# Eighteen down-projection units as seven block products instead of eight

## The reference

```python
# first block, per layer:
h = h + 0.5 * swiglu(rmsnorm(h, ffn1_norm), w_gate, w_up, w_down)       # D_FF = 2816
h = h + mixer(rmsnorm(h, mix_norm))
h = h + 0.5 * swiglu(rmsnorm(h, ffn2_norm), w_gate, w_up, w_down)
# second block, per layer:
mix = mixer_sublayer(x, ...)
x = layer_norm(DEEPNORM_ALPHA * x + mix, ln1_g, ln1_b)
ff = jnp.square(jax.nn.relu(x @ w_ff1)) @ w_ff2                         # D_FF_2 = 4096
x = layer_norm(DEEPNORM_ALPHA * x + ff, ln2_g, ln2_b)
```

## Time and profile before

| | |
|---|---|
| median of three runs | 2044.6 us |
| span of the profiled execution | 2042.5 us (the runs' median is 2.1 us above it) |
| PE busy | 2034.5 us, 10364 instructions |
| PE weight load busy | 1718.3 us |
| DVE busy | 1389.1 us |
| ACT busy | 1018.4 us |
| POOL busy | 92.8 us |
| granted TensorE clock | 1.000 of full speed |

### The profile page before, as it was taken

How to read it: one execution, slowest core, us unless ns; L and a number is a source line. 1 busy time by engine, 2 the same in 40 slices (tenths; PEclk the granted TensorE clock), 3 DMA queues, 4 the chain that set the end, 5 groups by cost and what they waited for, 6 DMA issues and landing times.

```text
span 2042.5 us, 25162 instructions
## 1 busy us (share of the span) xinstructions
PE 2034.5 (100%) x10364; PEld 1718.3 (84%) x10364; DVE 1389.1 (68%) x1624; ACT 1018.4 (50%) x1290; POOL 92.8 (5%) x133
## 2 busy tenths in 40 slices
PE   9999999999999999999999999999999999999998
PEld 7888888888888888888888888888888888888887
DVE  6655687775757566877675667757767677577675
ACT  6444576453445335775443365644444466445331
POOL 1001010000010001100100000000100000000000
PEclk9999999999999999999999999999999999999999
DMA  9655554465566656544656474555755656455552
GB/s 333 211 187 166 178 162 141 167 214 185 186 197 210 194 168 201 165 145 145 226 191 197 153 242 155 166 172 173 239 186 189 204 153 194 156 185 193 196 189 83
DMA packets 225569, 377.73 MB, mean 185 GB/s; under 512 B 6592, under 2 KB 113216, under 8 KB 225456
## 3 DMA queue, kind: packets, MB, share of 16 engines
q1 hardware_dynamic: 221472, 362.64, 54.1%
q0 software_dynamic: 3984, 13.49, 2.2%
HBM read 375.05 MB, written 1.05 MB: 184 GB/s over the span
## 4 chain that ended last, share of the span: by engine, by line
PE 98%; DVE 1%; ACT 0%; issue 0%; DVEq 0%; POOL 0%; ACTq 0%; POOLq 0%
PE pb L1656 63%; PE pb L1667 18%; PE pb L1670 9%; PE pb L1679 2%; PE pb L1725 1%; PE pb L1803 1%; DVE wl L2109 0%; PE pb L1802 0%; PE pb L1790 0%; PE pb L1860 0%; PE pb L1782 0%; PE pb L1645 0%; DVE lS L2292 0%; PE pb L1649 0%; PE pb L1647 0%; PE pb L1684 0%
## 5 line engine op out<-in xcount | busy, mean ns | idle before, releaser
L1891 ACT ACTIVATE wh<-raw 128x2048 fp32r<-128x2048 f32 (+2 forms) x347 | 654.2, 1886 | 626.6 <-PE pb L1656 271.3
L2109 DVE TENSOR_TENSOR wl<-raw,wh 128x2048 fp32r<-128x2048 f32 (+2 forms) x347 | 777.3, 2247 | 149.0 <-ACT wh L1891 147.8
L1656 PE MATMUL pb<-wh,x 128*128 128x512 f32 (+1 forms) x2144 | 651.3, 385 | 0.0
L1656 PEld LDWEIGHTS pb<-wh,x 128*128 128x128 f32 x2144 | 400.7, 188 | 77.9
L1656 PE MATMUL pb<-wl,x 128*128 128x512 f32 (+1 forms) x1072 | 421.1, 393 | 0.1
L1667 PE MATMUL pb<-x,wh 128*128 128x512 f32 x1568 | 397.0, 395 | 0.0
L1667 PEld LDWEIGHTS pb<-x,wh 128*128 128x128 f32 x1568 | 283.3, 189 | 51.8
L1656 PE MATMUL pb<-wl,mh 128*128 128x512 f32 (+1 forms) x740 | 255.7, 391 | 0.0
L1656 PE MATMUL pb<-wh,ml 128*128 128x512 f32 (+1 forms) x740 | 253.7, 388 | 0.0
L1656 PE MATMUL pb<-wh,mh 128*128 128x512 f32 (+1 forms) x740 | 253.5, 388 | 0.0
L1656 PEld LDWEIGHTS pb<-wl,x 128*128 128x128 f32 x1072 | 201.4, 188 | 42.2 <-issue 3.7
(11 more groups left out here) (365 smaller groups left out, 1611.8 us busy)
## 6 DMA issues: line engine op xcount, KB each, us to landing
raw<-in_w_in_dram SPq DMA_DIRECT2D x100, 1024.0 KB, 5.3
raw<-in_w_ff_dram SPq DMA_DIRECT2D x64, 1024.0 KB, 5.3
raw<-in_ffn_w_down_dram SPq DMA_DIRECT2D x44, 1024.0 KB, 4.9
raw<-in_ffn_w_up_dram SPq DMA_DIRECT2D x42, 1024.0 KB, 5.3
raw<-in_ffn_w_gate_dram SPq DMA_DIRECT2D x41, 1024.0 KB, 5.3
raw<-in_w_branch_dram SPq DMA_DIRECT2D x24, 1024.0 KB, 5.0
raw<-in_w_out_dram SPq DMA_DIRECT2D x16, 1024.0 KB, 5.0
raw<-in_w_in_dram SPq DMA_DIRECT2D x4, 832.0 KB, 4.4
```

The source lines that it names most:

```text
L1656: ins = e.matmul(pb[b][:, 0:c1 - c0], x[:, s, cols], w[:, n, c0:c1], start=(it["first"] and n == 0 and q == 0), stop=(it["stop"] and n == ...
L1891: e.activation(hi, raw, ACT.Copy).then_inc(m.high_done, 1)
L2109: e.tensor_tensor(lo, raw, hi.bitcast(F32), ALU.subtract).then_inc(m.low_done, 1)
```

## The change

`down` marks two units of each chunk (`seven_units`) as 2x2 blocks: left operand A split in token halves by K tiles, right operand B in K tiles by column halves. In place of eight block products there are seven, of sums of blocks of B (`sum`, four 128x512 pieces, made by DVE from the raw weights, split by ACT and DVE as `sumh`, `suml`) and sums and differences of blocks of A (`diff`, made by POOL from `mn`, split as `diffh`, `diffl`). Three products go straight to the main banks, four to the side banks, which both marked units of the chunk share; then `recombine` adds the side banks to `h` (one ACT copy, eight DVE instructions). The chunks are the first of the three `ffn1` calls after the opening one, and all three of both `ffn2` calls: nine chunks, 18 units.

A `diff` needs its hidden values in `mn` in the wide form. So in `ffn2`'s first chunk the second 512 columns, before in the tokens form, are now in the wide form, and the starting group has two units instead of four.

The side operands take memory that the mixer constants use, so `loads` is now called ahead of the last group of down units.

```diff
@@ advance / new helpers
         while self.nlo < self.nhi:
-            self.add("low", j=self.nlo)
+            n = self.seven.get(self.nlo)
+            if n is not None and n > 1 and n - 2 not in self.sum_free:
+                break
+            self.add("low", j=self.nlo, n=n, after=self.sum_free.get(n - 2) if n is not None else None)
             self.nlo += 1
+            self.sum_low_next()
+            if n is not None:
+                self.sum_high_due = n
...
+    def seven_products(self, j, job):
+        n, slots = self.next("seven"), job["slots"]
+        self.seven_of[j] = n
+        self.sum_high_next()
+        self.sum_low_next()
+        need = self.need("M", slots, [0, 1]) + self.need("D", [n], [0])
...
+        v = self.pe("seven", j=j, n=n, slots=slots, mains=mains, sides=self.side_uses, first=first,
+                    begin=job["seven"] == "first", end=job["end"], need=need)
...
+        if job["end"]:
+            r = self.next("recombined", 2)
+            self.add("recombine", p=v["p"], uses=self.side_uses, coef=job["coef"], n=r,
+                     need=self.h_ready[0] + self.h_ready[1])
...
@@ split_later: after a wide product
+            if slot // 2 in self.seven_units:
+                self.mn_free[q].append(self.differences(q, ("product", n + 1)))
+    def differences(self, q, need):
+        n = self.next("diff")
+        self.add("diff", q=q, n=n, need=need, after=self.sum_free.get(n - 2))
+        def high():
+            self.add("diffhigh", n=n, after=self.sum_free.get(n - 2))
+            self.later.append(low)
+        def low():
+            self.add("difflow", n=n)
+            self.ready["D", n, 0] = ("diff_low", n + 1)
+        self.later.append(lambda: self.later.append(high))
@@ ffn1
-        if loads:
-            loads()
+            self.seven_units = () if opening or n0 else (2, 3)
-            self.down(dn, l, n0, sum(chunks) // 256, sizes, 0.5, after if n0 else None)
+            self.down(dn, l, n0, sum(chunks) // 256, sizes, 0.5, after if n0 else None, loads=loads if n0 else None)
@@ ffn2
-        if loads:
-            loads()
-            first = 2 if n0 == 0 else 0
+            self.seven_units = (2, 3) if n0 == 0 else (0, 1)
+            first = 1 if n0 == 0 else 0
-                                 last=(i == 1), epi=self.relu_t(4 * c)) for c in range(2) for i in range(2)],
+                                 last=(i == 1), epi=self.relu_t(4 * c)) for c in range(first) for i in range(2)],
@@ PE
+        elif k == "seven":
...
+            pe.wait_ge(m.low_done, it["j"] + 1)
+            pe.all_ready(it["need"])
+            for x, y, k, (b, g), first, stop in (
+                    ([x[:, s0, T] for x in a], w, 0, q1, begin, it["end"]),
+                    ([x[:, s1, T] for x in a], w, 2, q2, b2, False),
+                    ([x[:, 3, :] for x in d], w, 3, q3, b3, False),
+                    ([x[:, 1, :] for x in d], v, 0, q5, begin, it["end"]),
+                    ([x[:, 0, :] for x in d], v, 1, q7, begin, it["end"]),
+                    ([x[:, 2, :] for x in d], v, 2, q6, begin, it["end"]),
+                    ([x[:, s1, U] for x in a], v, 3, q4, b4, False)):
+                if y is v:
+                    pe.wait_ge(m.sum_low, n + 1)
+                if first:
+                    pe.wait_ge(m.evac[b], g)
+                e.matmul(pb[b][:, :], x[0], y[1][:, k, :], start=first, stop=False)
+                e.matmul(pb[b][:, :], x[0], y[0][:, k, :], start=False, stop=False)
+                ins = e.matmul(pb[b][:, :], x[1], y[0][:, k, :], start=False, stop=stop)
@@ DVE
+                v.step(e.tensor_tensor(V[:, 0:2, :], B[:, 0:4:3, :], B[:, 1:2, :].broadcast_to([P, 2, 512]), ALU.add))
+                v.own_steps()
+                v.step(e.tensor_tensor(V[:, 2, :], V[:, 0, :], B[:, 3, :], ALU.add))
+                e.tensor_tensor(lo[:, 0:512], raw[:, 0:512], hi[:, 0:512].bitcast(F32), ALU.subtract)
...
+        elif k == "recombine":
...
+            v.pe(p)
+            v.all_ready(it["need"])
+            v.wait_ge(m.part_copied, n // 2 + 1)
+            e.tensor_tensor(E, Q6, W, ALU.add).then_inc(m.evac[q6[0]], 1)
+            e.scalar_tensor_tensor(h[0][0], Q1, c, h[0][0], ALU.mult, ALU.add).then_inc(m.evac[q1[0]], 1)
...
+            e.scalar_tensor_tensor(h[1][1], E, c, h[1][1], ALU.mult, ALU.add).then_inc(m.evac[q7[0]], 1)
```

More of the change, by code:

```diff
@@ L274, in sbuf @@
         self.chunk = A("chunk", o_ck, [P, P], U32)
+        o_sum, o_sumh = (o_xn, o_g[1]), (o_lane[0], o_r2)
+        self.sum = [A(f"sum{i}", o_sum[i], [P, 4, 512]) for i in range(2)]
+        self.suml = [A(f"suml{i}", o_sum[i], [P, 4, 512], F32R) for i in range(2)]
+        self.sumh = [A(f"sumh{i}", o_sumh[i], [P, 4, 512], F32R) for i in range(2)]
+        self.diff = [A(f"diff{i}", o_r2 + 8192 + 2048 * i, [P, 4, P]) for i in range(2)]
+        self.diffl = [A(f"diffl{i}", o_r2 + 8192 + 2048 * i, [P, 4, P], F32R) for i in range(2)]
+        self.diffh = [A(f"diffh{i}", o_r2 + 12288 + 2048 * i, [P, 4, P], F32R) for i in range(2)]
+        self.mix = [A(f"mix{i}", o_xn + 2048 * i, [P, 512]) for i in range(3)]
         self.lrR = A("lrR", o_dist, [P, S], F32R)
@@ L538, in group @@
             need = self.need(X, slots, [t])
-            if job["first"]:
-                for b, _, _ in job["segs"]:
+            if job.get("seven"):
+                if t == 0:
+                    self.seven_products(j, job)
+                self.tick()
+                continue
+            first = []
+            for b, _, _ in job["segs"]:
+                first.append((t, b) not in self.opened if job["first"] is None else job["first"])
+                if first[-1]:
                     self.main_use[t, b] = self.use(2 * t + b)
+                    self.opened.add((t, b))
             segs = [(self.main_use[t, b], c0, c1) for b, c0, c1 in job["segs"]]
@@ L692, in cut, with seven @@
                 after(1, 1)
+        def seven(i):
+            return ("first" if i == min(self.seven_units) else "next") if i in self.seven_units else None
         u = 0
+        self.opened = set()
         for size in sizes:
-            first, last = u == 0, u + size == n_units
+            last = u + size == n_units
+            if last and loads:
+                loads()
             if last and after:
@@ L705, in down @@
                                  slots=[2 * (u + i), 2 * (u + i) + 1], segs=[(0, 0, 512), (1, 512, 1024)],
-                                 first=first and i == 0, last=last and i == size - 1, epi=epi)
+                                 first=None, last=last and i == size - 1, epi=epi, coef=coef,
+                                 seven=seven(u + i), end=u + i == max(self.seven_units, default=None))
                             for i in range(size)])
@@ L870, in ffn2 @@
                     n_t += 1
[L871 removed]
+            self.down("w_ff2_2", l, n0, n_chunks * 2, sizes, 1.0, after if n0 == 2560 else None, n0 == 2560 and l == L - 1,
+                      loads if n0 == 2560 else None)
     def start(self):
@@ L1644, in pe_program @@
                     pe.wait_ge(m.x0_high, 1)
-                e.matmul(pb[b][:, :], xh[:, s, cols], hi[:, 0, :], start=it["first"], stop=False)
+                e.matmul(pb[b][:, :], xh[:, s, cols], hi[:, 0, :], start=it["first"][0], stop=False)
                 pe.all_ready(it["need"])
```

135 lines of the change are left out of this document (119 added, 16 removed).

## The result

The changed kernel takes 2085.8 us (median of four runs, 2084.9 to 2086.9); the kernel before, with one run more than above, takes 2044.7. That is a ratio of 1.020 (95% interval 1.019 to 1.022), 41.1 us slower. The profiled execution has a span of 2085.1, 42.6 above that of before.

The account below looks back on a forecast made before the run. PE was taken as the bound in every stage: -13.4 us of removed work, +40.6 of waits on DVE in ffn2 and +4 of clock gave +31.2 on 2044.6, so 2076 us, range 2050 to 2092.

Parts of the forecast that it names:

- B: ffn2's second chunk, first marked unit: PE waits for diffl because DVE lags behind added work; 7.5 us a layer.
- the second part of D: ffn2's third chunk: the sixth product waits for the bank that the last wadd frees; 2.1 us a layer.
- D: ffn2's third chunk: PE waits for side banks, 3.2 us at the first product and 2.1 at the sixth.
- A: Start of ffn2: with two t=0 blocks gone, the first t=1 block waits for DVE's x rows; 6.2 us a layer.
- POOL, for which I took 0: Differences made on POOL: 2.2 to 10.0 us each, 0 on the path and 0 taken from DVE.
- My upper bound of 4.4 a chunk: The most DVE time POOL's differences might take: 6 x 0.73 = 4.4 us a chunk, 17.6 in all.
- C: ffn2's third chunk: the last ml stands behind recombine, two t=0 blocks cover 5.46 of 6.8 us; 1.3 left.
- The clock: Stretches at half clock behind PE's longer pauses in ffn2: four pauses at 1.0 us each, +4, ends 0 and 16.
- PE, removed: 54 matmuls fewer in 18 units (12.3 us), 16 transposes dropped (1.6), wide blocks +0.5: net -13.4 us.
- rows 10: Mixer trace: a POOL operation took 3.34 us around a DVE subtraction of usual 2.28, its equal 0.73; POOL seemed to wait.
- The second rival: Clock falls at A, B and D in both layers (+16 instead of +4), or POOL holds DVE back; 2088, chance 0.11.
- Loads at 0: The moved transfers cost POOL 3.8 us where nothing waits, data wanted over 20 us later: 0, uncovered 3.8.

Follow-up runs that it names:

- mains first: Changed kernel with a marked unit's three main-bank products ahead of its four side-bank ones, the difference awaited only before its first use; 2082.0 us.
- the best version: Changed kernel with mains first, differences two blocks earlier, recombine behind the last ml, ten marked units (six in ffn1, none in ffn2's first chunk); 2038.75 us.

## Why the prediction was right, and where it was off

- **The mechanism.** PE is the bound, so DVE's work costs only where PE waits for it, and there in full. Four waits were named with their places, and all four are there. Their sum is 38.2 where 40.6 stood; that it came so close is partly luck, since B was 3.0 too short and the second part of D, 4.2, too much (both layers).
- **A**: 6.2 forecast, 5.0 and 0.7 ahead of the turn measured. The run without marks shows that the missing t=0 blocks alone make it.
- **B**: 7.5 forecast, 9.0 measured. 1.3 of the 1.5 is POOL, for which I took 0: DVE's two-input operations were held back by 0.14 to 0.27 us each. The Trainium skill (SBUF — State Buffer, "SBUF: two separate sides") has this as a lock, by which a GpSimd operation that reads SBUF also makes a DVE instruction with two SBUF inputs wait. The run with fills in place of the differences agrees with it: DVE's times are the usual ones and B is 1.3 shorter. My upper bound of 4.4 a chunk held.
- **D**: 3.2 and 2.1 forecast, 3.3 and nothing measured. The second part showed (1.5) once the clock stayed up. **C**: 1.3 forecast, 1.0 measured; no run tests it alone.
- **The clock** is the term that was mis-sized: +4 forecast, 14.8 measured. The step that failed has two parts: that a pause must reach 4.8 us to cost anything, read from the end of the kernel, and that the price is 1.0 each because DVE's lateness would hide the rest. In the profile after, 1.9 us into D's pause the clock was still whole, and then it fell; one of 3.0 (mains first) did it too, pauses of 1.0 to 1.5 did not. Each fall cost 1.7 to 3.0 us there, and 1.4 to 3.1 in the other runs. The idle matmuls gained 10.3 of the 14.8 back, so even net of what DVE hides the term was too small. The Trainium skill (TensorE: Matmul & The Clock Gate, "What's actually happening") says that the throttled clock is the default state and that activity releases it. The trace agrees as far as each of the pauses A, B and D was followed by a stretch at half clock.
- **PE, removed**: -13.4 forecast. Two sentences of the prediction gave the wrong share: a unit gains 0.68 us (three matmuls), not 1.36, and a chunk of `ffn1` 1.36, not 2.7. The sum had it right. Measured were 1.2 a chunk, since in a marked unit matmuls start every 0.231 us and not 0.2275 (378 x 0.0035 = 1.3 us in all).
- **The sum**: -13.4 + 1.3 + 38.2 + 14.8 = +40.9; the medians differ by 41.1. The spans differ by 42.6: 0.7 of the rest arises in the opening, ahead of the first marked unit, and some 1 us stays unexplained.
- **The forecast** of 2076 was 10 us low, by the 10.8 of the clock. The second rival had the clock at A, B and D in both layers, and its 2088 lies nearer: there +16 was the right size, and it was given a chance of only 0.11 because D was thought too short and rows 10 showed DVE not slowed. Loads at 0 were right, and no wait on ACT's new work shows.

What stays open: what makes the same pause cost 1.5 us of clock once and 3 another time, and whether the best version needs mains first (the rows give it 1.4 us of margin, but no run leaves it out).

## What to carry to other kernels

When the bound engine has no slack, work put on another engine is to be placed, not averaged: DVE had 653 us idle in all, and yet 7 us of sums ahead of one 0.7 us instruction that frees a PSUM bank cost PE 4.6 us. In the nearly full chunks one marked unit with an unmarked one ahead of it gained 0.4 to 0.55 us, and two at the front lost. A pause of PE of 3 us or more had a second price of 1.4 to 3.1 us in the clock, so count both for each stall.

## What the runs showed of the hardware

- The granted clock fell behind pauses of 3.0 to 9.0 us (once behind one of 2.4, with one of 1.7 close ahead of it) and stayed whole behind those of up to 1.5; work at half clock (0.43 between starts of 512 columns, 0.23 at full) followed for up to 6 us after PE had resumed. Matmuls that compute nothing kept it up and made the kernel 10.3 us faster.
- DVE and POOL slowed each other: DVE's 2048-wide split took 2.54 beside a `diff` and 2.28 otherwise, POOL's 128-column step 2.39 and 0.80. With short fills in place of POOL's reads both effects were gone.
- A rotation of PSUM banks turned a change in one chunk into a wait of 8.65 in place of 3.3 us two chunks later; that the banks are the cause is read from the kernel's order and the matching 5.6 us between the two `wadd`.
